# Reciprocal roots taken for two tiles at once and a new list schedule in the first layer's start, on 8 cores of a Trainium2 chip

## The chip, the cores and the metric

The kernel runs on the 8 cores of one Trainium2 chip, with the batch split over them. Each core has TensorE (PE, with its weight loads PEld), VectorE (DVE), ScalarE (ACT), GpSimd (POOL), and SyncE (SP), which issues DMA transfers. The time is that of the slowest core, in microseconds (us).

## The reference, cut to what matters

Four layers, each of this form; D_MODEL is 1024, each core has 16 prompt tiles and one sample tile of 128 tokens (17 tiles, numbered 0 to 16).

```python
h = rmsnorm(x, pre_g)                       # x * rsqrt(mean(x*x) + eps) * g
proj = einsum('bld,de->ble', h, w_in)       # columns u, v, z_a, p, z_b, xc, bg, cg, z_c
a_out, vn = chunk_gmlp(u, v, v_g, w_s, b_s) # vn = rmsnorm(v, v_g), v is 768 wide
b_out, new_pool = pool_mixer(p, ...)
c_out, new_conv = short_conv(xc, bg, cg, ...)
mix = concat([a_out * silu(z_a), b_out * silu(z_b), c_out * silu(z_c)])
x = x + rmsnorm(einsum('ble,ed->bld', mix, w_out), post_g)
```

## The kernel before, in words

The change touches only what each core does in layer 0 before its big projections start: for each of the 17 tiles, load x, normalise it, transpose it, multiply it with the v columns of w_in, and normalise the result into vn. After that come the stages of layer 0 (first the one of branch A), in which TensorE hardly ever waits, and the same again for layers 1 to 3, which are not touched.

The steps of tile j in this start, by the names that `plan_first` gives them, with engine and line of the kernel before:

- sq: ACT squares x and sums it up (L426, output `sb_samp`).
- rs: POOL adds eps (L446) and raises to the power -0.5 (L448); two instructions on one column of `stats`.
- nm: DVE multiplies x with this root and the gain into one of three buffers `hbuf` (L434).
- tp and ev: PE transposes the buffer in eight 128x128 pieces (L505), and DVE or ACT copies the result from PSUM to `hT` (L515 on DVE, L426 with output `sb_hT` on ACT). From tile N_PE_T on there is instead dt, a DMA transpose issued by SP (L518), straight from `hbuf` to `hT`.
- mm: 16 matmuls, eight pairs of 512 and 256 columns, into two PSUM banks (L528). For the first KOUT tiles they are planned as eight separate pieces mk, one for each of the eight parts of the weights w_v as these land.
- vs, vr, vn: ACT squares the product (L426, output `sb_ar`), POOL takes the root (L446, L448), DVE writes vn (L561, output `sb_mix`; the sample tile 16 goes by L434 to `sb_ar`).

Each engine runs its instructions strictly in the order written. That order is the list that `plan_first` makes: at each turn the step that could start first by its table of durations and landing times (`land_x`, `land_w`). `vbank` gives the PSUM banks: a tile's mm must wait until vn of the tile that had the banks before is done. nm of tile j waits until tile j-3 has left its `hbuf` buffer, by tp or by the landing of dt.

SP issues the loads of the x tiles in order, tile 16 once nm 4 is done, and after nm 6 in the program five loads that later stages need: `pscale`, `fac`, `convw` (8 to 36 KB), `sc_in` (480 KB) and the bias rows `b_sp` (384 KB, into `post_bc`). The DMA transposes come behind these in SP's queue. POOL issues loads too: the weight tiles `w_t` into `ring`, each behind a fixed vn (tiles 4, 5, 8 and 12 to 16), and the spatial weights `w_sp` and `w_spd` behind vn 6. Behind vn 9 DVE prepares the first weight pair (three additions, L641), behind vn 10 it masks the spatial weights, and behind vn 11 to 14 it forms sums of `hT` blocks.

Of the kernel before, what the change touches and what calls it, by code (L numbers as in the profile page):

```python
# [73 lines left out]

def plan_first():


# [9 lines left out]
    user = {}  # L87
    for j in range(NT):
        step(("sq", j), {"ACT": 1.25}, [], j + 0.0, land_x[j])
        step(("rs", j), {"POOL": 1.1}, [(("sq", j), 0.0)], j + 0.0)  # L90
# [24 lines left out]
        step(("vr", j), {"POOL": 1.1}, [(("vs", j), 0.0)], j + 1.2)  # L115
        step(("vn", j), {"DVE": 1.02}, [(("vr", j), 0.1)], j + 1.3)
    while steps:
        best = None
        for name, (engs, deps, lead, t0) in steps.items():
# [7 lines left out]
            if best is None or (t, lead) < best[0]:  # L127
                best = ((t, lead), name, eng, t + engs[eng])
        _, name, eng, end = best
# [90 lines left out]
def build_nc():  # L220
# [35 lines left out]
    with ExitStack() as es:  # L256
# [187 lines left out]
        def rstd(si):  # L444
            col = stats[:, si:si + 1]
            emit(POOL, lambda g: g.tensor_scalar(out=col, in0=col, scalar1=EPS, scalar2=None, op0=ALU.add),  # L446
                 reads=[R_stat[si]], writes=[R_stat[si]])
            emit(POOL, lambda g: g.tensor_tensor(out=col, in0=col, in1=neghalf[:], op=ALU.pow),  # L448
                 reads=[R_stat[si], R["neghalf"]], writes=[R_stat[si]])
            return col  # L450
# [1070 lines left out]
```

How the kernel before makes its waits and increments, by code:

```python
def emit(q, fn, reads=(), writes=(), dsem=None, extra=()):  # L173
# [15 lines left out]
        add(w.w)  # L189
        for tok in w.r.values():
            add(tok)
    for tok in extra:
        add(tok)
    for k, (s, v) in deps.items():
        if q.is_pe and s is q.sem:
            continue
        if q.waited.get(k, 0) >= v:
            continue
        q.h.wait_ge(s, v)
        q.waited[k] = v
    ins = fn(q.h)
    if dsem is not None:
        dsem.count += 16
        ins.then_inc(dsem.sem, 16)
        tok = (dsem.sem, dsem.count)
    else:
        q.count += 1
        ins.then_inc(q.sem, 1)
        tok = (q.sem, q.count)
    for w in writes:
        w.w = tok
# [8 lines left out]
def build_nc():  # L220
# [1225 lines left out]
            sp_dma(post_bc[:], post_g[l], [], [R["post"]], d_c["post"])  # L1446
            c_stage(l, pr)
            sp_dma(nsc_p[l], stc[:].rearrange("p a b -> p (a b)"), [R["stc"]], [], d_out)
            job = b_stage(l)
            if not last:
                load_wpg(l + 1)
            job.run()
        for dsm in d_xst + [d_out]:
            if dsm.count:
                nc.sync.wait_ge(dsm.sem, dsm.count)
    return nc
```

## Time and profile before

| what | us |
|---|---|
| median of 3 runs (lowest, highest) | 1872.65 (1869.07, 1872.83) |
| the profiled execution, its own time | 1868.77 |
| its span, from the first to the last instruction of its slowest core (7) | 1867.3 |
| spans of the eight cores in it | 1860.6 to 1867.3 |
| PE busy on core 7 | 1827.0 (98%) |
| DVE busy on core 7 | 1539.9 (82%) |

In a timeline row the first number is the start and the second how long the row lasts (several instructions of one kind are merged as "xN"); in square brackets stands how long the engine had been idle before, and what ended that.

### The profile page before, as it was taken

What the parts mean: (1) busy time and instruction counts of PE and PEld (TensorE: products, weight loads), DVE (VectorE), ACT (ScalarE), POOL (GpSimd) and SP (SyncE); (2) the same over time, 40 slices, a digit from 0 to 9 for tenths busy, and PEclk for the clock granted to TensorE, in tenths of its full rate; (3) what the DMA queues carried; (4) which work ended last, traced back from release to release, by engine and by line L of the source; (5) the groups of instructions that cost most, each with busy time, mean ns of one, the idle gap of its engine ahead of it and who ended that gap; (6) DMA issues with size and microseconds to landing.
All of it is one profiled execution on the core that took longest, in us unless ns stands there. A gap on an engine that the chain in (4) does not pass through costs nothing.

```text
span 1867.3 us, 33678 instructions; the slowest of 8 cores (1860.6 to 1867.3 us)
## 1 busy us (share of the span) xinstructions
PE 1827.0 (98%) x10048; PEld 902.7 (48%) x10048; DVE 1539.9 (82%) x2420; ACT 901.0 (48%) x1743; POOL 392.3 (21%) x698
## 2 busy tenths in 40 slices
...
GB/s 249 121 40 53 46 46 67 119 115 200 191 105 40 56 36 43 88 99 124 232 186 79 41 55 46 40 108 104 141 236 151 39 51 40 36 72 114 74 162 166
DMA packets 130979, 187.16 MB, mean 100 GB/s; under 512 B 70385, under 2 KB 76145, under 8 KB 130802
## 3 DMA queue, kind: packets, MB, share of 16 engines
...
q8 instruction: 85, 1.39, 0.3%
...
HBM read 198.79 MB, written 42.35 MB: 129 GB/s over the span
## 4 chain that ended last, share of the span: by engine, by line
PE 90%; DVE 2%; DMA 2%; issue 2%; POOL 2%; ACT 1%; SPq 0%; DVEq 0%; ACTq 0%; POOLq 0%
PE ps L656 46%; PE ps L1163 18%; PE ps L455 16%; PE ps L528 7%; PE ps L1175 1%; PE ps L747 1%; DMA sb_mix<-w_v 1%; POOL sb_stats L448 1%; PE ps L1059 1%; DVE sb_ar L434 1%; DMA sb_ar<-x_in 1%; ACT sb_ar L426 1%; DMA x_mid<-sb_ar 1%; DVE sb_ar L430 0%; POOL sb_stats L446 0%
## 5 line engine op out<-in xcount | busy, mean ns | idle before, releaser
L426 ACT ACTIVATE sb_ar<-ps 128x512 f32<-128x512 f32 (+3 forms) x774 | 489.9, 639 | 605.7 <-PE ps L656 350.5
L455 PE MATMUL ps<-sb_hT,sb_ring 128*128 128x128 bf16 (+1 forms) x2432 | 333.9, 286 | 0.2 <-DVE sb_mix L561 0.2
L656 PE MATMUL ps<-sb_wout,sb_ring 128*128 128x512 bf16 x1152 | 295.6, 379 | 0.0
L656 PE MATMUL ps<-sb_hT,sb_ring 128*128 128x512 bf16 x1152 | 295.6, 379 | 0.0
L392 POOL DMA_DIRECT2D sb_ring<-w_t x176 | 96.3, 547 | 860.1 <-PE ps L656 387.3
L430 DVE TENSOR_TENSOR sb_ar<-sb_ar 128x512 f32<-128x512 f32 (+5 forms) x332 | 256.8, 774 | 23.2 <-DVE sb_ar L430 12.9
L455 PEld LDWEIGHTS ps<-sb_hT,sb_ring 128*128 128x128 bf16 x2432 | 191.3, 98 | 154.0 <-issue 0.6
L528 PE MATMUL ps<-sb_mix,sb_hT 128*128 128x512 bf16 x1088 | 186.1, 333 | 16.7 <-DVE sb_hT L515 6.7
L1163 PE MATMUL ps<-sb_wout,sb_mix 128*128 128x512 bf16 x768 | 178.2, 379 | 4.4 <-DVE ps L1113 4.3
L448 POOL TENSOR_TENSOR sb_stats<-sb_stats,sb_neghalf 128x1 f32<-128x1 f32 x204 | 167.4, 821 | 30.6 <-POOL sb_stats L446 1.0
L656 PE MATMUL ps<-sb_wout,sb_tex 128*128 128x512 bf16 x672 | 172.4, 379 | 1.2 <-DVE sb_tex L641 1.2
L656 PEld LDWEIGHTS ps<-sb_hT,sb_ring 128*128 128x128 bf16 x1152 | 109.6, 98 | 121.2 <-issue 0.4
L430 DVE TENSOR_TENSOR sb_ar<-ps,sb_ar 128x512 f32<-128x512 f32 x240 | 163.9, 683 | 4.5 <-PE ps L656 4.4
L434 DVE SCALAR_TENSOR_TENSOR sb_ar<-sb_pcx,sb_convw,sb_ar 128x512 f32<-128x512 f32 x192 | 140.0, 749 | 24.4 <-ACT sb_ar L849 14.1
L656 PEld LDWEIGHTS ps<-sb_wout,sb_ring 128*128 128x128 bf16 x1152 | 106.7, 98 | 103.2 <-issue 0.7
L446 POOL TENSOR_SCALAR sb_stats<-sb_stats 128x1 f32<-128x1 f32 x204 | 70.9, 347 | 392.4 <-ACT sb_ar L426 302.7
L528 PEld LDWEIGHTS ps<-sb_mix,sb_hT 128*128 128x128 bf16 x1088 | 107.5, 100 | 93.4 <-issue 25.8
L656 PE MATMUL ps<-sb_wout,sb_hbuf 128*128 128x512 bf16 x480 | 123.1, 379 | 0.9 <-DVE sb_hbuf L641 0.9
L426 ACT ACTIVATE ps<-ps 128x512 f32<-128x512 f32 x176 | 103.5, 588 | 40.8 <-PE ps L1163 20.6
L1163 PEld LDWEIGHTS ps<-sb_wout,sb_mix 128*128 128x128 bf16 x768 | 74.7, 98 | 96.9 <-issue 8.9
L434 DVE SCALAR_TENSOR_TENSOR sb_ar<-ps,sb_stats,sb_post_bc 128x1024 f32<-128x1024 f32 x68 | 87.2, 1282 | 38.6 <-POOL sb_stats L448 22.4
L426 ACT ACTIVATE sb_samp<-ps 128x128 f32<-128x128 f32 (+1 forms) x152 | 61.9, 407 | 99.9 <-PE ps L1163 97.6
(115 smaller groups left out, 2191.5 us busy)
## 6 DMA issues: line engine op xcount, KB each, us to landing
...
```

Of the source, the lines that this page charges most:

```text
L392: emit(POOL, lambda g: g.dma_start(out=flat, in_=a.src), writes=a.res, dsem=d_ring[pos])
L426: return emit(ACT, lambda a: a.activation(out=out, in_=in_, func=func, scale=scale, **kw), reads=reads, writes=writes, extra=extra)
L430: return emit(DVE, lambda v: v.tensor_tensor(out=out, in0=in0, in1=in1, op=op), reads=reads, writes=writes)
L434: return emit(DVE, lambda v: v.scalar_tensor_tensor(out=out, in0=in0, scalar=scalar, in1=in1, op0=op0, op1=op1), reads=reads, writes=writes)
L446: emit(POOL, lambda g: g.tensor_scalar(out=col, in0=col, scalar1=EPS, scalar2=None, op0=ALU.add), reads=[R_stat[si]], writes=[R_stat[si]])
L448: emit(POOL, lambda g: g.tensor_tensor(out=col, in0=col, in1=neghalf[:], op=ALU.pow), reads=[R_stat[si], R["neghalf"]], writes=[R_stat[si]])
L455: ins = pe.matmul(bank(b, n), lhsT=wa.ap[:, k, :], rhs=hT[:, k, c0:c0 + n], start=(k == 0), stop=(k == 7))
L528: ins = pe.matmul(ps[:, 512 * (b + bo):512 * (b + bo) + n], lhsT=hT[:, k, j * 128:(j + 1) * 128], rhs=wv.ap[:, k, c0:c0 + n], start=(k == ...
L656: ins = pe.matmul(bank(b), lhsT=lhs[:, k, :], rhs=rhs[0][:, k, :], start=(first and k == 0), stop=(k == 3), skip_group_check=not first)
L747: ins = pe.matmul(ps[:, 512 * b + jj * 128:512 * b + (jj + 1) * 128], lhsT=vn[:, j0 + jj, h * 128:(h + 1) * 128], rhs=wsrc[:, h, :], start ...
L1059: emit(PE, lambda pe: pe.matmul(bank(b, n), lhsT=wpg[:, gi, :], rhs=dd, start=True, stop=True), reads=[rm, R["wpg"]], writes=[bank_res[b]])
L1163: ins = pe.matmul(bank(b), lhsT=lhs[0][:, k, :], rhs=rhs[:, k, :], start=(first and k == 0), stop=(k == 7), skip_group_check=not first)
```

## The change

- POOL's rs is taken for two tiles at once: tiles 0 to 4 singly, then (5, 6), (7, 8), (9, 10), (11, 12), (13, 14), (15, 16). The two instructions then work on two neighbouring columns; the tiles' sums have fixed columns of their own in `stats`.
- One tile fewer goes through TensorE's transpose: N_PE_T is 9, so tile 9 is transposed by DMA, and the banks of tiles 9 to 16 are given anew.
- Only tiles 0 and 1 have their mm in pieces (KOUT is 2). Tile 2's 16 matmuls follow as one.
- The planner has other landing times and durations, and a penalty of 0.3 on nm in its choice, so the order on every engine is another.

```diff
-N_PE_T = 10
 XSLOTS = 12
-KOUT = 3
+KOUT = 2
+N_PE_T = 9
+PEN = {"nm": 0.3}
 def vbank(j):
-    return 2 * (j % 3) if j < N_PE_T else (6, 2, 4, 0, 2, 6, 4)[j - N_PE_T]
+    return 2 * (j % 3) if j < N_PE_T else (0, 6, 2, 4, 0, 2, 6, 4)[j - N_PE_T]
+def x_pairs():
+    return [(j,) for j in range(5)] + [(j, j + 1) for j in range(5, NT, 2)]
...
-        step(("rs", j), {"POOL": 1.1}, [(("sq", j), 0.0)], j + 0.0)
+        if j == pair_of[j][0]:
+            step(("rs", j), {"POOL": 1.15}, [(("sq", i), 0.1) for i in pair_of[j]], j + 0.0)
...
-            ready = (("dt", j), 3.0)
+            ready = (("dt", j), 3.5)
...
-            if best is None or (t, lead) < best[0]:
-                best = ((t, lead), name, eng, t + engs[eng])
+            key = (t + PEN.get(name[0], 0.0), lead)
+            if best is None or key < best[0]:
+                best = (key, name, eng, t, t + engs[eng])
...
-        def rstd(si):
-            col = stats[:, si:si + 1]
+        def rstd(si, n=1):
+            col = stats[:, si:si + n]
...
-                rstd(stat_of[j])
+                rstd(NSTAT + j, next(len(p) for p in x_pairs() if j in p))
```

What this moves, at three places. All lines of the changed kernel are 8 higher here (L434 is ACT's helper there, L442 is nm, L523 ev, L569 vn).

ACT from tile 0 to tile 7, before: sq has the output `sb_samp,sb_stats`, vs has `sb_ar,sb_stats`, ev has `sb_hT`.

```order
L426 ACTIVATE sb_samp,sb_stats<-sb_ar 128x1024 x4
L426 ACTIVATE sb_ar,sb_stats<-ps 128x768 x3
L426 ACTIVATE sb_samp,sb_stats<-sb_wout 128x1024 x3
L426 ACTIVATE sb_ar,sb_stats<-ps 128x768
L426 ACTIVATE sb_samp,sb_stats<-sb_wout 128x1024 x4
L426 ACTIVATE sb_ar,sb_stats<-ps 128x768
L426 ACTIVATE sb_samp,sb_stats<-sb_wout 128x1024
L426 ACTIVATE sb_ar,sb_stats<-ps 128x768
L426 ACTIVATE sb_hT<-ps 128x8x128
```

And now:

```order
L434 ACTIVATE sb_samp,sb_stats<-sb_ar 128x1024 x4
L434 ACTIVATE sb_samp,sb_stats<-sb_wout 128x1024
L434 ACTIVATE sb_ar,sb_stats<-ps 128x768 x3
L434 ACTIVATE sb_hT<-ps 128x8x128
L434 ACTIVATE sb_samp,sb_stats<-sb_wout 128x1024 x3
L434 ACTIVATE sb_ar,sb_stats<-ps 128x768
L434 ACTIVATE sb_samp,sb_stats<-sb_wout 128x1024
L434 ACTIVATE sb_ar,sb_stats<-ps 128x768
```

sq 4 stands ahead of the first three vs; ev 3 is ACT's, where ACT had ev 7 before; vs 4 comes after sq 8 and no longer after sq 10.

DVE from tile 3 on, before: nm 3, vn 0, ev 3, vn 1 and 2, nm 4 and 5, ev 4, vn 3, ev 5, nm 6 to 8, vn 4, ev 6.

```order
L434 SCALAR_TENSOR_TENSOR sb_hbuf<-sb_ar,sb_stats,sb_pre_bc 128x1024
L561 SCALAR_TENSOR_TENSOR sb_mix<-ps,sb_stats,sb_vb_bc 128x768
L515 COPY sb_hT<-ps 128x8x128
L561 SCALAR_TENSOR_TENSOR sb_mix<-ps,sb_stats,sb_vb_bc 128x768 x2
L434 SCALAR_TENSOR_TENSOR sb_hbuf<-sb_wout,sb_stats,sb_pre_bc 128x1024 x2
L515 COPY sb_hT<-ps 128x8x128
L561 SCALAR_TENSOR_TENSOR sb_mix<-ps,sb_stats,sb_vb_bc 128x768
L515 COPY sb_hT<-ps 128x8x128
L434 SCALAR_TENSOR_TENSOR sb_hbuf<-sb_wout,sb_stats,sb_pre_bc 128x1024 x3
L561 SCALAR_TENSOR_TENSOR sb_mix<-ps,sb_stats,sb_vb_bc 128x768
L515 COPY sb_hT<-ps 128x8x128
```

And now: nm 3, nm 4, vn 0, ev 4, vn 1 and 2, nm 5 and 6, vn 3, ev 5 and 6, vn 4, nm 7 to 9, vn 5, ev 7 and 8.

```order
L442 SCALAR_TENSOR_TENSOR sb_hbuf<-sb_ar,sb_stats,sb_pre_bc 128x1024
L442 SCALAR_TENSOR_TENSOR sb_hbuf<-sb_wout,sb_stats,sb_pre_bc 128x1024
L569 SCALAR_TENSOR_TENSOR sb_mix<-ps,sb_stats,sb_vb_bc 128x768
L523 COPY sb_hT<-ps 128x8x128
L569 SCALAR_TENSOR_TENSOR sb_mix<-ps,sb_stats,sb_vb_bc 128x768 x2
L442 SCALAR_TENSOR_TENSOR sb_hbuf<-sb_wout,sb_stats,sb_pre_bc 128x1024 x2
L569 SCALAR_TENSOR_TENSOR sb_mix<-ps,sb_stats,sb_vb_bc 128x768
L523 COPY sb_hT<-ps 128x8x128 x2
L569 SCALAR_TENSOR_TENSOR sb_mix<-ps,sb_stats,sb_vb_bc 128x768
L442 SCALAR_TENSOR_TENSOR sb_hbuf<-sb_wout,sb_stats,sb_pre_bc 128x1024 x3
L569 SCALAR_TENSOR_TENSOR sb_mix<-ps,sb_stats,sb_vb_bc 128x768
L523 COPY sb_hT<-ps 128x8x128 x2
```

ev 6 now stands ahead of the three nm that it stood behind.

DVE from nm 12 on, now (nm 12, vn 7, nm 13, vn 8, nm 14, vn 9, the weight pair, nm 15, vn 10, the two masks, nm 16, vn 11):

```order
L442 SCALAR_TENSOR_TENSOR sb_hbuf<-sb_ar,sb_stats,sb_pre_bc 128x1024
L569 SCALAR_TENSOR_TENSOR sb_mix<-ps,sb_stats,sb_vb_bc 128x768
L442 SCALAR_TENSOR_TENSOR sb_hbuf<-sb_ar,sb_stats,sb_pre_bc 128x1024
L569 SCALAR_TENSOR_TENSOR sb_mix<-ps,sb_stats,sb_vb_bc 128x768
L649 TENSOR_TENSOR sb_tex<-sb_ring 128x512
L649 TENSOR_TENSOR sb_tex<-sb_tex,sb_ring 128x512
L649 TENSOR_TENSOR sb_tex<-sb_ring,sb_tex 128x512
L442 SCALAR_TENSOR_TENSOR sb_hbuf<-sb_ar,sb_stats,sb_pre_bc 128x1024
L569 SCALAR_TENSOR_TENSOR sb_mix<-ps,sb_stats,sb_vb_bc 128x768
L438 TENSOR_TENSOR sb_wmt<-sb_wmt,sb_cstb 128x768
L438 TENSOR_TENSOR sb_bdt<-sb_bdt,sb_cstb 128x768
L442 SCALAR_TENSOR_TENSOR sb_hbuf<-sb_wout,sb_stats,sb_pre_bc 128x1024
```

The same stretch before, from the weight pair on: nm 16 followed nm 15 at once, ahead of vn 10 and the masks.

```order
L641 TENSOR_TENSOR sb_tex<-sb_ring 128x512
L641 TENSOR_TENSOR sb_tex<-sb_tex,sb_ring 128x512
L641 TENSOR_TENSOR sb_tex<-sb_ring,sb_tex 128x512
L434 SCALAR_TENSOR_TENSOR sb_hbuf<-sb_ar,sb_stats,sb_pre_bc 128x1024
L434 SCALAR_TENSOR_TENSOR sb_hbuf<-sb_wout,sb_stats,sb_pre_bc 128x1024
L561 SCALAR_TENSOR_TENSOR sb_mix<-ps,sb_stats,sb_vb_bc 128x768
L430 TENSOR_TENSOR sb_wmt<-sb_wmt,sb_cstb 128x768
L430 TENSOR_TENSOR sb_bdt<-sb_bdt,sb_cstb 128x768
L561 SCALAR_TENSOR_TENSOR sb_mix<-ps,sb_stats,sb_vb_bc 128x768
```

On SP the row of DMA transposes has eight instructions where it had seven, still behind the load of `b_sp`.

## Rows read from the trace of the kernel before

**Rows 1.** Spans of all cores: us, mean granted TensorE clock.

```profile
core 3: 1866.2 us, clock 0.996
core 4: 1866.1 us, clock 0.997
core 7: 1867.3 us, clock 0.996
```

**Rows 2.** Core 7 by stage: width, busy us of each engine, clock, DMA share, GB/s.

```profile
24.00:53.00 29.00, 20.97 (x143) 12.44 (x141) 20.11 (x21) 21.00 (x42) 22.24 (x42) 0.88 0.94 264
53.00:79.00 26.00, 24.23 (x148) 14.19 (x147) 21.84 (x24) 8.40 (x19) 17.39 (x26) 1.00 0.78 110
```

**Rows 3.** Timeline of core 7, TensorE, 23 to 79 us.

```profile
23.66 1.13 PE L528 MATMUL ps<-sb_mix,sb_hT 128*128 128x512 bf16 x6 [0.27 <-DMA sb_mix<-w_v]
26.18 0.61 PE L505 MATMUL ps<-sb_cstb,sb_hbuf 128*128 128x128 bf16 x8 [1.38 <-DVE sb_hbuf L434]
28.87 4.24 PE L528 MATMUL ps<-sb_mix,sb_hT 128*128 128x512 bf16 x16 [2.08 <-DVE sb_hT L515]
...
34.61 5.40 PE L528 MATMUL ps<-sb_mix,sb_hT 128*128 128x512 bf16 x32 [0.61 <-DVE sb_hT L515]
...
44.36 7.04 PE L528 MATMUL ps<-sb_mix,sb_hT 128*128 128x512 bf16 x32 [3.46 <-DVE sb_hT L515]
...
52.79 13.16 PE L528 MATMUL ps<-sb_mix,sb_hT 128*128 128x512 bf16 x80 [0.50 <-DVE sb_hT L515]
...
70.48 7.96 PE L528 MATMUL ps<-sb_mix,sb_hT 128*128 128x512 bf16 x48 [1.20 <-DVE sb_mix L561]
78.28 1.03 PE L656 MATMUL ps<-sb_hT,sb_ring 128*128 128x512 bf16 x4
```

**Rows 4.** Timeline of core 7, VectorE, GpSimd and ScalarE, 24 to 42 us.

```profile
24.74 1.28 DVE L434 SCALAR_TENSOR_TENSOR sb_hbuf<-sb_ar,sb_stats,sb_pre_bc 128x1024 bf16<-128x1024 f32 x1 [5.43 <-POOL sb_stats L448]
...
25.30 0.80 POOL L446 TENSOR_SCALAR sb_stats<-sb_stats 128x1 f32<-128x1 f32 x1 [0.73 <-ACT sb_ar L426]
...
27.00 1.02 DVE L561 SCALAR_TENSOR_TENSOR sb_mix<-ps,sb_stats,sb_vb_bc 128x768 bf16<-128x768 f32 x1 [0.97 <-POOL sb_stats L448]
...
27.93 0.68 DVE L515 COPY sb_hT<-ps 128x1024 bf16<-128x1024 bf16 x1
...
31.88 1.39 POOL L448 TENSOR_TENSOR sb_stats<-sb_stats,sb_neghalf 128x1 f32<-128x1 f32 x1
...
41.38 1.02 ACT L426 ACTIVATE sb_hT<-ps 128x1024 bf16<-128x1024 bf16 x1
```

**Rows 5.** Core 7: SP's issues, issues with KB and us to landing, the DMA transposes.

```profile
32.11 0.62 SPq L439 DMA_DIRECT2D sb_pscale<-pscale  x1
...
34.44 0.44 SPq L439 DMA_DIRECT2D sb_post_bc<-b_sp  x1
...
sb_post_bc<-b_sp SPq DMA_DIRECT2D x1, 384.0 KB, 13.8
...
sb_pscale<-pscale SPq DMA_DIRECT2D x1, 8.0 KB, 12.5
...
DMA to landing us min/median/max: 2.8/4.2/6.6
```

**Rows 6.** Core 4: the same views (TensorE, SP, us to landing).

```profile
53.27 13.16 PE L528 MATMUL ps<-sb_mix,sb_hT 128*128 128x512 bf16 x80 [1.49 <-DVE sb_hT L515]
...
78.55 1.03 PE L656 MATMUL ps<-sb_hT,sb_ring 128*128 128x512 bf16 x4
...
34.97 1.46 SPq L439 DMA_DIRECT2D sb_post_bc<-b_sp  x1
49.65 19.47 SPq L518 DMA_TRANSPOSE sb_hT<-sb_hbuf  x7
...
sb_post_bc<-b_sp SPq DMA_DIRECT2D x1, 384.0 KB, 17.2
...
sb_hT<-sb_hbuf SPq DMA_TRANSPOSE x1, 4.7
```

More of the change, by code:

```diff
@@ L87, in plan_first @@
     user = {}
+    pair_of = {j: p for p in x_pairs() for j in p}
     for j in range(NT):
         step(("sq", j), {"ACT": 1.25}, [], j + 0.0, land_x[j])
-        step(("rs", j), {"POOL": 1.1}, [(("sq", j), 0.0)], j + 0.0)
-        gone = [] if j < NHB else [((("tp" if j - NHB < N_PE_T else "dt"), j - NHB), 0.0 if j - NHB < N_PE_T else 3.0)]
-        step(("nm", j), {"DVE": 1.28}, [(("rs", j), 0.1)] + gone, j + 0.0)
+        if j == pair_of[j][0]:
+            step(("rs", j), {"POOL": 1.15}, [(("sq", i), 0.1) for i in pair_of[j]], j + 0.0)
+        gone = [] if j < NHB else [((("tp" if j - NHB < N_PE_T else "dt"), j - NHB), 0.0 if j - NHB < N_PE_T else 3.5)]
+        step(("nm", j), {"DVE": 1.22}, [(("rs", pair_of[j][0]), 0.1)] + gone, j + 0.0)
         b = vbank(j)
@@ L97, in plan_first @@
             step(("tp", j), {"PE": 0.6}, [(("nm", j), 0.1)] + ([(("ev", j - 2), 0.1)] if j >= 2 else []), j + 0.2)
-            step(("ev", j), {"DVE": 0.7, "ACT": 1.05}, [(("tp", j), 0.1)], j + 0.3)
+            step(("ev", j), {"DVE": 0.65, "ACT": 1.0}, [(("tp", j), 0.1)], j + 0.3)
             ready = (("ev", j), 0.1)
@@ L101, in plan_first @@
             step(("dt", j), {"SP": 1.3}, [(("nm", j), 0.1)], j + 0.3)
-            ready = (("dt", j), 3.0)
-            if j == N_PE_T:
+            ready = (("dt", j), 3.5)
+            if b == 6 and j < NT - 2:
                 old = [(("ev", N_PE_T - 1), 0.1), (("ev", N_PE_T - 2), 0.1)]
@@ L114, in plan_first @@
         step(("vs", j), {"ACT": 1.0}, [(last, 0.1)], j + 1.2)
-        step(("vr", j), {"POOL": 1.1}, [(("vs", j), 0.0)], j + 1.2)
-        step(("vn", j), {"DVE": 1.02}, [(("vr", j), 0.1)], j + 1.3)
+        step(("vr", j), {"POOL": 1.15}, [(("vs", j), 0.0)], j + 1.2)
+        step(("vn", j), {"DVE": 0.95}, [(("vr", j), 0.1)], j + 1.3)
     while steps:
```

30 lines of the change are left out of this document (14 added, 16 removed).

## The prediction, made before the changed kernel ran

> **What bounds the kernel now.** I read the busy shares first: TensorE is busy nearly all of the span, so a change can only help where it waits. The stages show one such stretch before layer 0's own stages: from 24 to 53 us core 7's PE is busy 20.97 of 29.00 us at a granted clock of 0.88; from 53 to 79 us it is busy 24.23 of 26.00 at full clock [rows 2]. The change acts on these 55 us. PE's timeline then shows the waits: 2.08 us before tile 3, 0.61 before tile 4, 3.46 before tile 6, 0.50 before tile 8, all for ev, the copy of the transposed tile [rows 3]. The clock: 16 matmuls of tile 3 take 4.24 us, 32 of tiles 6 and 7 take 7.04, against 13.16/5 = 2.63 us a tile in the row of 80 [rows 3]. So two stretches run partly at half speed (1.2 GHz), each behind an idle stretch, and cost 1.6 and 1.8 us. From tile 8 on PE is nearly the bound: tile 9 begins at 52.79+2.63 = 55.4, eight tiles of 2.63 would end at 76.5, the first matmul of the next stage comes at 78.28 [rows 3]. The last 1.8 us are waits, among them 1.20 for a vn that stands late on DVE.
>
> What ends the waits is the order on the engines. ev 3 copies a tile that PE had transposed at 26.79, but stands behind vn 0 on DVE and starts at 27.93; vn 0 itself waited for vr 0, whose first POOL instruction took 0.80 us beside nm 3 [rows 3, 4].
>
> **The change part by part, on core 7.** I walk each engine's new order with the durations of the rows: nm 1.28, vn 1.02, ev 0.68 on DVE and 1.02 on ACT [rows 4], tp 0.53, tile 2.63.
>
> Tiles 2 to 4. The last part of w_v lands as now. Tiles 0 and 1 have four matmuls left (0.65 us), then all 16 of tile 2 follow: 23.66+0.65+2.63 = 26.9. That is 10 matmuls more behind the landing than the 6 now [rows 3]; they fill time in which PE idles anyway (1.38 and 2.08). tp 3 ends at 27.5. ev 3 on ACT comes behind vs 2: 27.9 to 28.9. rs 4 stands beside nm 3 and comes out at 26.8, nm 4 ends at 28.2, vn 0 at 29.1, and tile 3 needs the latter's bank: it starts at 29.2, 0.3 later than now. It then runs with tile 4 behind it, without the low clock: 29.2+5.3 = 34.5. Now tile 4 only starts at 34.61. So 2.7 us are won by here.
>
> Tiles 5 and 6. The pair step rs (5, 6) waits for sq 6, at 31.3; nm 5 and 6 end at 34.9, vn 3 at 35.8, ev 5 at 36.5, tile 5 starts at 36.6, tile 6 ends at 42.0. Now tile 6 starts at 44.36 and the low clock follows.
>
> Tiles 7 and 8. vn 5 ends at 43.4, ev 7 at 44.0, tiles 7 and 8 run from 44.3 to 49.6. Now tile 8 ends at 55.4: **5.8 us won by here**, 3.4 of them the two low-clock stretches, the rest waits.
>
> The power of two columns is not in the trace. From below it costs what one column does, 0.22+0.15+0.57 = 0.94 us with its addition; from above two of those, 1.88. I take 0.95, because the one row I have is far from a cost per element at width 1, and keep 0.9 us on the path for the upper end (it would delay nm 5, and with it tile 5). A POOL step beside an nm is longer: the power took 1.39 [rows 4]. The Trainium skill's page GPSIMD Engine Reference, section 1, says GpSimd's memory interface is shared with VectorE, with contention when VectorE has two SBUF inputs; by that the pairs nm 5/6 and nm 7 to 9 stretch vr 3 and rs 9 as nm 3 does vr 0, and the trace agrees. Without it tile 3 would start some 0.6 earlier; the sum here has it in.
>
> Tile 9 is the step at which I stop believing in the 5.8. Its dt is issued at about 41.6, when nm 9 is done; the first dt of the kernel before is issued at 49.65 on core 4 [rows 6], when the loads are nearly in. `pscale`, 8 KB, is issued at 32.11 and lands 12.5 us later, behind the x tiles issued before it; `b_sp` is issued at 34.44 and lands at 48.2 [rows 5]. SP's transfers come out in the order in which they went in. So dt 9 can't land before `b_sp`. On core 4 `b_sp` lands at 34.97+17.2 = 52.2, and the first dt, issued at 49.65, lands at 54.35, 2.2 behind it [rows 6]; the median transpose of core 7 lands 4.2 behind its issue [rows 5]. I take 2.0 behind `b_sp`, since dt 9 will have been queued longest (bounds 1 and 4.2). And `b_sp` itself comes later: the two spatial weight loads (0.38 MB) go out behind vn 6 at about 47, not at 51.7, which at 264 GB/s [rows 2] is up to 1.5 us; I take 0.8.
>
> Core 7: tile 9 starts at 48.2+0.8+2.0 = 51.0, not at 49.6. Core 4: 52.2+2.8 = 55.0, where tile 9 starts at 53.27+2.63 = 55.9 now [rows 6]: of its gain by tile 8 (it would end there at about 51.5) only 0.9 is left.
>
> From tile 9 on. Eight tiles take 21.0. nm 12 waits for the buffer of tile 9, so it starts when dt 9 lands, and behind it on DVE stand vn 7, nm 13, vn 8, nm 14, vn 9, the weight pair, nm 15, vn 10, the masks, nm 16 and vn 11: five nm at 1.2, five vn at 0.94 (they overlap by 0.09), 1.8 and 1.0, together 13.5 to 13.9. Tile 14 needs the bank that vn 11 frees and would start 13.2 after tile 9. So 0.3 to 0.7 of waiting, and I take 0.7, against 1.8 now (1.6 on core 4). vs, vr and vn of tile 16 are as now, and so are the stages after it, where PE is the bound (98% of the span busy); what is won at the end of tile 16 stays won.
>
> **The sum.** Core 7: 51.0+21.0+0.7 = 72.7 against 78.28: 5.6 less, 1867.3 becomes 1861.7. Core 4: 55.0+21.7 = 76.7 against 78.55: 1.8 less, 1866.1 becomes 1864.3. Core 3, with 1866.2 now [rows 1], lies between. So the slowest core is another one: the span falls from 1867.3 to 1864.3, by **3.0 us**. The profiled execution (1868.77) would take 1865.8; the median of the runs is 3.9 above that execution, so the forecast is 1872.65-3.0 = **1869.6**.
>
> **The rivals.**
> 1. *The DMA transposes are not held by the loads.* Then core 4 goes on from 51.5: 51.5+21.7 = 73.2, 5.3 less, 1860.8, core 7 72.7-1.4 = 71.3, 7.0 less, 1860.3. Span 1860.8, 6.5 less: 1866.2. For it: a transpose may start beside the loads' last packets on another of the 16 engines; on core 7 loads land earliest. Against it: the 12.5 us of an 8 KB load. In the Trainium skill, DMA: Bandwidth & Descriptors, section Queues, rings and completion order, completion is said not to be first in, first out for one issuing engine, although each ring is consumed in order; by its first half this rival would hold, by its second the forecast.
> 2. *The clock falls in the new gap.* On core 4 PE would idle from 51.5 to 55.0. The 3.46 us of idle before tile 6 were followed by half clock on core 7, at a cost of 1.8 [rows 3]. Then core 4 gains nothing, 1866.1, 1.2 less than now: 1871.5.
> 3. *Slower.* The queued transposes come out one by one: dt 9 4.2 behind `b_sp`, dt 10 and 11 each 2.8 later (the shortest landing [rows 5]). On core 4: dt 9 at 57.2, dt 11 at 62.8, nm 14 only then; vn 9, weight pair, nm 15, vn 10, masks, nm 16, vn 11 need 9.1 more, tile 14 starts at 71.9 and tile 16 ends at 79.8, 1.3 later than now, and 3.1 later with the clock of rival 2. Core 4: 1869.2, which is 1.9 above now: 1874.5. It decides from the point at which dt 9 lands 5 us behind `b_sp` or dt 11 10 us behind. For it: landings of up to 6.6 [rows 5]. Against it: core 4's 2.2.
>
> **How the numbers follow.** Forecast 0.50, its own range 1.5 to 4.7 less (`b_sp` delayed by 0 to 1.5, dt 9 1 to 3 behind it, two-column power at its upper end where covered). Rival 1: 0.23. Rival 2: 0.17. Rival 3: 0.10. A measurement of this kernel can't tell less than about 0.2% (3.7 us) from no change. Of the forecast's case 0.17 lies beyond that, and nearly all of rival 1; of rival 3, with the runs' own spread of 3.8 [the table of times], 0.06. Faster 0.40, same 0.54, slower 0.06. The range of 1864.5 to 1873.3 leaves out the far side of rival 1 and of rival 3.
>
> **What would show it.** Right: PE's tiles 3 and 4 back to back without low clock; tile 8 ending at about 50 to 52; then an idle stretch on PE ended by the DMA into `hT`, longest on the cores where `b_sp` lands last, and nm 12 waiting for the same; the power on two columns at about 0.57. Wrong: tile 9 directly behind tile 8 (rival 1), half clock behind the gap (rival 2), waits for each of tiles 9 to 11 (rival 3). All of it falls if `b_sp` lands before 46, or if tile 5 waits longer for its pair than computed, since sq 6 needs a tile that lands late on some cores.

## The result, and the profile after

The changed kernel takes 1877.28 us (median of 20 runs), the kernel before 1872.93 in runs beside it. The ratio is 1.0025, with a 95% interval of 1.0015 to 1.0034: **slower by 0.25%, about 4.7 us**. The medians take in all runs, the ratio only the fast ones, in which no die ran long at a lower clock. I had forecast 3.0 us less. The execution profiled took 1876.2 us. Its spans, which answer to [rows 1]:

```profile
core 0: 1860.6 us, clock 0.998
core 1: 1869.7 us, clock 0.995
core 2: 1861.0 us, clock 0.997
core 3: 1870.0 us, clock 0.995
core 4: 1861.7 us, clock 0.998
core 5: 1869.6 us, clock 0.995
core 6: 1874.9 us, clock 0.994
core 7: 1862.8 us, clock 0.997
```

Four cores (0, 2, 4, 7) are at 1861 to 1863, the other four at 1870 to 1875 with a lower clock. In this execution that split makes most of the time lost. In other executions other cores are the late ones: the median span over the executions lies between 1864.2 and 1869.9 for each of the eight cores.

I begin with the two cores of the forecast. Core 7 by stage, as in [rows 2]:

```profile
24.00:53.00 29.00, 23.73 (x156) 14.21 (x157) 21.21 (x22) 21.02 (x42) 17.80 (x32) 0.89 1.06 272
53.00:79.00 26.00, 23.68 (x143) 13.60 (x142) 21.06 (x23) 8.79 (x19) 15.60 (x25) 1.00 0.80 124
```

TensorE is busier between 24 and 53 us than before (23.73 against 20.97), but the granted clock is hardly better (0.89 against 0.88). Where the low clock lies now is seen in core 7's TensorE timeline, as in [rows 3].

```profile
22.59 0.81 PE L536 MATMUL ps<-sb_mix,sb_hT 128*128 128x512 bf16 x4 [2.04 <-DMA sb_mix<-w_v]
24.53 6.30 PE L536 MATMUL ps<-sb_mix,sb_hT 128*128 128x512 bf16 x20 [1.14 <-DMA sb_mix<-w_v]
...
33.05 5.36 PE L536 MATMUL ps<-sb_mix,sb_hT 128*128 128x512 bf16 x32 [1.33 <-ACT sb_hT L434]
...
41.27 5.36 PE L536 MATMUL ps<-sb_mix,sb_hT 128*128 128x512 bf16 x32 [1.53 <-DVE sb_hT L523]
...
49.13 7.96 PE L536 MATMUL ps<-sb_mix,sb_hT 128*128 128x512 bf16 x48 [1.61 <-ACT sb_samp L434]
57.87 10.56 PE L536 MATMUL ps<-sb_mix,sb_hT 128*128 128x512 bf16 x64 [0.78 <-DMA sb_hT<-sb_hbuf]
68.95 5.36 PE L536 MATMUL ps<-sb_mix,sb_hT 128*128 128x512 bf16 x32 [0.52 <-DVE sb_mix L569]
75.33 2.76 PE L536 MATMUL ps<-sb_mix,sb_hT 128*128 128x512 bf16 x16 [1.01 <-DMA sb_hT<-sb_hbuf]
77.92 1.03 PE L664 MATMUL ps<-sb_hT,sb_ring 128*128 128x512 bf16 x4
```

The waits up to tile 8 are smaller, as forecast: 1.33, 1.53, 1.61 before tiles 3, 5, 7, where 2.08, 0.61, 3.46 and 0.50 stood. But the 20 matmuls behind the last part of w_v (four of tiles 0 and 1, 16 of tile 2) take 6.30 us. On core 4 they take 3.41:

```profile
24.08 3.41 PE L536 MATMUL ps<-sb_mix,sb_hT 128*128 128x512 bf16 x20 [1.07 <-DMA sb_mix<-w_v]
...
46.12 5.36 PE L536 MATMUL ps<-sb_mix,sb_hT 128*128 128x512 bf16 x31 [1.56 <-DVE sb_hT L523]
56.15 14.61 PE L536 MATMUL ps<-sb_mix,sb_hT 128*128 128x512 bf16 x78 [4.67 <-DMA sb_hT<-sb_hbuf]
71.54 8.24 PE L536 MATMUL ps<-sb_mix,sb_hT 128*128 128x512 bf16 x47 [0.78 <-DVE sb_mix L569]
79.61 1.03 PE L664 MATMUL ps<-sb_hT,sb_ring 128*128 128x512 bf16 x4
```

Core 4 goes as forecast up to tile 8, which ends at 51.5. Then TensorE waits 4.67 us for the first DMA transpose (to 56.15, forecast 55.0), and the next stage starts at 79.61, where it started at 78.55 [rows 6].

Core 1 is one of the four late cores:

```profile
48.88 5.36 PE L536 MATMUL ps<-sb_mix,sb_hT 128*128 128x512 bf16 x32 [1.60 <-ACT sb_samp L434]
61.69 5.28 PE L536 MATMUL ps<-sb_mix,sb_hT 128*128 128x512 bf16 x16 [7.45 <-DMA sb_hT<-sb_hbuf]
68.03 10.56 PE L536 MATMUL ps<-sb_mix,sb_hT 128*128 128x512 bf16 x64 [1.06 <-DMA sb_hT<-sb_hbuf]
...
87.60 1.03 PE L664 MATMUL ps<-sb_hT,sb_ring 128*128 128x512 bf16 x4
```

TensorE idles 7.45 us, and tile 9's 16 matmuls take 5.28 us instead of 2.6. The stages of core 1, columns as in [rows 2]:

```profile
50.00:55.00 5.00, 4.24 (x27) 2.35 (x24) 2.48 (x3) 3.04 (x7) 3.99 (x8) 1.00 1.17 192
55.00:60.00 5.00, 0.00 (x0) 0.00 (x0) 0.00 (x0) 0.24 (x2) 1.34 (x3) 0.68 1.39 86
60.00:65.00 5.00, 3.31 (x11) 1.60 (x12) 2.21 (x2) 0.00 (x0) 0.00 (x0) 0.50 1.45 107
65.00:70.00 5.00, 3.94 (x20) 1.81 (x18) 2.01 (x2) 0.90 (x2) 1.66 (x2) 0.80 1.24 148
```

From 55 to 60 us TensorE and VectorE do nothing at all, and the granted clock falls (0.68, then 0.50). The DMA's share of busy time is at its highest (1.39 and 1.45), while it moves the least (86 and 107 GB/s): packets are in flight, but slow. Core 1's waits between 24 and 92 us (us in total, times, the longest) say who waited:

```profile
DVE sb_hbuf L442 <- DMA sb_hT<-sb_hbuf: 13.3, 2, 8.9
...
PE ps L536 <- DMA sb_hT<-sb_hbuf: 9.0, 3, 7.5
```

VectorE loses more than TensorE: nm 12 and nm 13 need the `hbuf` buffers that dt 9 and dt 10 hold until they land. Last, what else was in the DMA queues. Issues of core 1 with the us from issue to landing, each row from a narrow stretch around its issue, at 38.01 (`b_sp`), 47.99 (the second `w_t` tile, issued by GpSimd) and 46.14 (dt 9):

```profile
sb_post_bc<-b_sp SPq DMA_DIRECT2D x1, 384.0 KB, 17.3
...
sb_ring<-w_t POOLq DMA_DIRECT2D x1, 256.0 KB, 12.1
sb_hT<-sb_hbuf SPq DMA_TRANSPOSE x1, 15.1
```

So `b_sp` lands at 55.3, the `w_t` tile at 60.0 and dt 9 at 61.2. On core 7 the same transpose took 4.9 us:

```profile
sb_hT<-sb_hbuf SPq DMA_TRANSPOSE x1, 4.9
```

All cores, from the traces (us; "half clock" is how long the low clock lasts from the gap before tile 9 on, "tile 16 ends" is the start of its vn less the 2.3 us between):

| core | tile 8 ends | b_sp lands | 2nd w_t tile lands | dt 9 lands | behind b_sp | half clock | tile 16 ends, before | after | span, after less before |
|---|---|---|---|---|---|---|---|---|---|
| 0 | 53.1 | 50.6 | 55.1 | 55.1 | 4.5 | 0 | 78.3 | 78.6 | -0.1 |
| 1 | 54.2 | 55.3 | 60.0 | 61.2 | 5.9 | 10.2 | 79.2 | 87.8 | +4.2 |
| 2 | 55.2 | 51.4 | 54.8 | 52.5 | 1.1 | 0 | 81.4 | 77.0 | -3.0 |
| 3 | 52.5 | 56.3 | 57.4 | 63.2 | 6.9 | 13.7 | 77.9 | 88.3 | +3.8 |
| 4 | 51.5 | 50.0 | 55.6 | 55.8 | 5.8 | 3.4 | 78.8 | 79.9 | -4.4 |
| 5 | 54.2 | 54.8 | 59.8 | 60.4 | 5.6 | 10.2 | 77.9 | 87.6 | +8.7 |
| 6 | 53.7 | 53.9 | 59.4 | 59.4 | 5.5 | 13.6 | 77.5 | 88.9 | +14.3 |
| 7 | 54.5 | 50.2 | 54.7 | 51.3 | 1.1 | 0 | 78.5 | 78.2 | -4.5 |

Tile 16 ends at 83.3 on average where it ended at 78.7, though tile 8 ends 2.5 earlier (53.6 against 56.1). The lead or lag that a core has at the start of vn 16 stays the same to 0.3 us through 770 us, on every core but core 7 of before, so what is lost in the first 90 us stays lost. The span differs from it because single cores lose a few us in the middle of the kernel. In the execution of before core 7 loses 5.8 us between 450 and 485 us against all the others, and cores 1, 3 and 4 lose 3.6, 5.2 and 4.2 between 900 and 1000 us. After, cores 2, 6 and 7 lose 1.9, 4.1 and 2.6 behind 900 us. The cores without such a slip take 1779.4 to 1780.8 us from the start of vn 16 to their end, before and after alike. Core 7's slip in the execution of before, at a change of layer, is this:

```profile
494.99 4.21 PE L528 MATMUL ps<-sb_mix,sb_hT 128*128 128x512 bf16 x16 [3.96 <-DVE sb_ar L434]
```

VectorE had waited for a DMA transpose there, too. So the slowest core of before, core 7 with 1867.3, was the slowest by such a slip, in layers that the change doesn't touch; core 6, the slowest after, had both the late dt 9 and a slip. That slips like this hide half of what the late cores lose in the other executions too (9 to 11 us on four cores become 4.7 of the time) is argued, not shown.

### The profile page after: what moved, and what is told of

It reads as the page before. It is cut to its first block, busy times and chain, and to the rows that moved or that the text cites. A ratio compares the mean times of both kernels' runs of the same rounds, so it can differ in the third digit from the quotient of the medians.

```text
span 1874.9 us, 33612 instructions; the slowest of 8 cores (1860.6 to 1874.9 us)
## 1 busy us (share of the span) xinstructions
PE 1828.9 (98%) x10040; PEld 903.3 (48%) x10040; DVE 1538.3 (82%) x2419; ACT 901.1 (48%) x1743; POOL 392.6 (21%) x686
## 3 DMA queue, kind: packets, MB, share of 16 engines
q8 instruction: 85, 1.39, 0.3%
## 4 chain that ended last, share of the span: by engine, by line
PE 87%; DVE 3%; issue 3%; DMA 3%; POOL 2%; ACT 1%; DVEq 0%; SPq 0%; ACTq 0%; POOLq 0%
PE ps L664 45%; PE ps L1171 16%; PE ps L463 16%; PE ps L536 6%; PE ps L1183 1%; PE ps L755 1%; POOL sb_stats L457 1%; DMA sb_mix<-w_v 1%; DMA sb_hT<-sb_hbuf 1%; DVE sb_ar L442 1%; PE ps L1067 1%; DVE sb_ar L438 1%; ACT sb_ar L434 1%; DMA x_mid<-sb_ar 1%; DVE sb_hbuf L442 0%
## 5 line engine op out<-in xcount | busy, mean ns | idle before, releaser
L434 ACT ACTIVATE sb_ar<-ps 128x512 f32<-128x512 f32 (+3 forms) x774 | 489.9, 639 | 607.6 <-PE ps L664 351.8
L457 POOL TENSOR_TENSOR sb_stats<-sb_stats,sb_neghalf 128x1 f32<-128x1 f32 (+1 forms) x198 | 171.0, 864 | 29.7 <-POOL sb_stats L455 0.6
L442 DVE SCALAR_TENSOR_TENSOR sb_ar<-sb_pcx,sb_convw,sb_ar 128x512 f32<-128x512 f32 x192 | 139.9, 749 | 24.2 <-ACT sb_ar L857 14.2
L455 POOL TENSOR_SCALAR sb_stats<-sb_stats 128x1 f32<-128x1 f32 (+1 forms) x198 | 67.4, 341 | 400.9 <-ACT sb_ar L434 311.5
L434 ACT ACTIVATE ps<-ps 128x512 f32<-128x512 f32 x176 | 103.5, 588 | 41.7 <-PE ps L1171 21.2
L442 DVE SCALAR_TENSOR_TENSOR sb_ar<-ps,sb_stats,sb_post_bc 128x1024 f32<-128x1024 f32 x68 | 87.2, 1282 | 37.9 <-POOL sb_stats L457 19.6
L434 ACT ACTIVATE sb_samp<-ps 128x128 f32<-128x128 f32 (+1 forms) x152 | 61.8, 407 | 100.6 <-PE ps L1171 98.3
```

The lines of the kernel that those rows point to most:

```text
L434: return emit(ACT, lambda a: a.activation(out=out, in_=in_, func=func, scale=scale, **kw), reads=reads, writes=writes, extra=extra)
L442: return emit(DVE, lambda v: v.scalar_tensor_tensor(out=out, in0=in0, scalar=scalar, in1=in1, op0=op0, op1=op1), reads=reads, writes=writes)
```

## The experiments

All kernels compute the whole result. I had three questions: which part of the change costs, what delays dt 9, and what is left once it isn't delayed. My theory (T in the expectations) was that tile 9's transpose comes while loads are still in flight and crawls; later I narrowed it to the loads of GpSimd's queue beside it (Q). The rivals were that SP's own loads ahead of it hold it, that the spatial weights do (S), and that the pairs or the new order do the harm (P). "Tile 16" below is the mean end of tile 16 over the eight cores, and the highest; it is 78.7 and 81.4 before, 83.3 and 88.9 after. Ratios are to the kernel before, with the 95% interval, from 4 to 11 runs of each kernel. Landings and "tile 16" are read from one execution of each kernel, and loads land some us apart from one execution to the next.

### Which part costs

**Ten TensorE transposes again**, all else as changed:

```diff
-N_PE_T = 9
+N_PE_T = 10
-    return ... else (0, 6, 2, 4, 0, 2, 6, 4)[j - N_PE_T]
+    return ... else (6, 2, 4, 0, 2, 6, 4)[j - N_PE_T]
```

> The changed kernel with ten TensorE transposes again (N_PE_T 10, the old banks, list made by the changed planner); everything else as changed. Theory T (the transpose of tile 9 goes out while the loads are still landing, so it and the two behind it crawl and TensorE waits for them): tile 9 needs no DMA, the first DMA transpose is issued 4 us later and is needed 2.6 us later; the stage of branch A begins on core 1, 3, 5 and 6 at 74 to 80 us instead of 87.5 to 88.5, and the kernel is 3 to 6 us faster than the one before. Rival P (the pairs and the new order on VectorE lose the time): still slower than before by 2 to 6 us. Rival S (the spatial weights, loaded earlier, are the cause): little change from the changed kernel, landings of DMA transposes stay at up to 15 us.

Measured: 0.9993 (0.9979 to 1.0007), tile 16 at 76.9 and 78.9. The loss is gone, and tile 16 ends 1.8 before that of the kernel before; the time shows no clear gain, where I had expected 3 to 6 us. The first DMA transpose is dt 10, which lands at 52 to 58 on the cores; tile 9 covers the wait.

**Nine in the kernel before**, the same two lines the other way (and the matching condition for the banks):

> The kernel before with nine TensorE transposes alone (its own landing table, single roots; its list made anew). Theory T: tile 9's DMA transpose goes out at about 46 to 49 us, close to the last loads; slower than the kernel before by 1 to 5 us, with landings over 8 us for tiles 9 and 10 on some cores. Rival P: same as the kernel before within 1 us, since the pairs aren't there.

Measured: 1.0000 (0.9990 to 1.0011), tile 16 at 80.0 and 84.1. The mechanism is there, the loss of time that I expected is not seen. On all eight cores dt 9 lands within 0.2 us of the second `w_t` tile (58.9 and 58.9, 54.1 and 54.0, 56.8 and 56.8, 59.6 and 59.5, 53.4 and 53.6, 59.9 and 60.0, 56.5 and 56.4, 54.7 and 54.8), and 4.6 to 8.4 us behind `b_sp`. Core 5, issues at 46.59 and 45.91 (us to landing), and its TensorE:

```profile
sb_ring<-w_t POOLq DMA_DIRECT2D x1, 256.0 KB, 13.4
sb_hT<-sb_hbuf SPq DMA_TRANSPOSE x1, 14.0
```

```profile
60.12 7.01 PE L528 MATMUL ps<-sb_mix,sb_hT 128*128 128x512 bf16 x32 [4.74 <-DMA sb_hT<-sb_hbuf]
```

Here tile 8 ends later (54.8 to 58.7): on five cores dt 9 is there by then, on three TensorE waits 2.3 to 4.7 us. So harm of the changed kernel's size came only with both parts of the change: the earlier tile 8 makes a longer gap of a transpose that is late in both.

**Pairs alone** in the kernel before (its constants, banks and N_PE_T; list made anew):

```diff
+def x_pairs():
+    return [(j,) for j in range(5)] + [(j, j + 1) for j in range(5, NT, 2)]
```

> The kernel before with the pairs alone: ten TensorE transposes, its own landing times and durations, three tiles in pieces, the list made anew with pair roots. Both theories: the DMA transposes go out as before, so nothing crawls; the end of tile 8 moves by less than 2 us from 55.3 to 56.1, and the kernel stays within 2 us of the one before. If the pairs themselves cost (rival P), 2 us or more slower.

Measured: 0.9995 (0.9981 to 1.0009), tile 16 at 78.1 and 79.9, tile 8 ending at 54.1 to 58.1 (before: 55.2 to 59.1), 56.1 on average in both. The pairs alone cost nothing that is seen; they are not the loss.

### What delays the transpose

**SP's five later loads behind the last transpose**, `b_sp` first among them:

```diff
-                if j == 6:
-                    sp_dma(pscale[:], ...)   # and fac, convw, sc_in, b_sp
...
+            elif kind == "dt":
+                t_job(j, j % NHB)
+                if j == NT - 1:
+                    sp_dma(post_bc[:, 0:768], b_sp[0], ...)   # and the other four
```

> The changed kernel, but the five loads for later stages (pscale, fac, convw, sc_in, b_sp; 0.9 MB) are issued behind the last DMA transpose instead of behind nm 6. Theory T: the queue is free of them when tile 9's transpose is issued at 44 to 46 us, which then waits only for the last x tiles (45 to 47) and lands by 50 to 52; the stage of branch A begins at 73 to 77 us on all cores, kernel 3 to 7 us faster than before. Rival S: the transposes still meet the weight loads of GpSimd's queue and land 10 to 15 us behind their issue. Rival P: no change from the changed kernel.

Measured: 0.9980 (0.9970 to 0.9990), tile 16 at 76.3 and 83.7. dt 9 lands at 47 to 51, before it is needed. So SP's own loads do hold it: with them out of the way it no longer waits. It was not slowed much by GpSimd's queue either: on all eight cores the second `w_t` tile went out 1.9 us behind dt 9, and dt 9 took 3.6 to 5.1 us and landed ahead of it. But not all is gone. On core 3 dt 10 was issued at 51.5, beside a `w_t` tile (in flight to 55.6) and the spatial weights (to 61.4 and 62.2), and took this:

```profile
sb_hT<-sb_hbuf SPq DMA_TRANSPOSE x1, 10.8
```

```profile
62.38 21.20 PE L536 MATMUL ps<-sb_mix,sb_hT 128*128 128x512 bf16 x112 [4.52 <-DMA sb_hT<-sb_hbuf]
```

With no load of SP's left to blame, the transpose lands with `w_spd` of GpSimd's queue, at 62.2; the half clock follows (seven tiles in 21.20 us, not 18.4).

**Spatial weights behind vn 9** instead of vn 6:

```diff
-                elif j == 6:
+                elif j == 9:
                     load_spatial(0)
```

> The changed kernel, but the two spatial weight loads are issued behind vn 9 instead of vn 6. Rival S: the transposes land 4 to 7 us behind their issue, and the kernel is 3 to 6 us faster than before. Theory T: tile 9's transpose still lands no sooner than the load of b_sp (50 to 55 us) and at most 2 us are won on the changed kernel.

Measured: 1.0024 (0.9996 to 1.0051), tile 16 at 78.9 and 84.3. The interval is too wide for a word on the time; one run of 1895 us makes it so, the other eight in it lie between 1867.7 and 1873.4. dt 9 still lands with the `w_t` tile on three cores (59.9 and 59.8, 57.3 and 57.3, 53.6 and 53.6), so the spatial weights are not what delays dt 9; dt 10 now comes about 1 us behind dt 9 on five cores and 3.2 to 3.5 on three, where it came 4 to 8 us behind it on the late cores, on three of them within 0.2 us of `w_spd`. So they do delay dt 10.

**`w_t` tiles earlier and spatial weights later**: the second `w_t` tile is in (46.3 to 49.9) before `b_sp` is, so that hardly a load of GpSimd's is left beside dt 9, while SP's loads stay ahead of it.

```diff
-                if j in (4, 5, 8, 12, 13, 14, 15, 16):
+                if j in (2, 3, 8, 12, 13, 14, 15, 16):
                     ring_try()
-                elif j == 6:
+                elif j == 9:
                     load_spatial(0)
```

> The changed kernel, but no load of GpSimd's queue is near the transposes of tiles 9 to 11: the first two weight tiles are issued behind vn 2 and 3 (about 32 and 36 us), the spatial weights behind vn 9; the five later loads stay ahead of the transposes on SP's queue. Theory Q (a transpose crawls while a load of GpSimd's queue is in flight beside it; the two land together): tile 9's transpose lands within 3 us of the load of b_sp, at 51 to 54 us, the next ones within 2 us of each other, and the stage of branch A begins at 74 to 78 us on all cores; 2 to 5 us faster than the kernel before. Theory T alone (the loads ahead in SP's own queue): landings at 55 to 63 us as in the changed kernel, on some cores.

Measured: 0.9994 (0.9980 to 1.0008), tile 16 at 79.4 and 84.4. dt 9 lands 0.9 to 2.5 us behind `b_sp` on all eight cores and dt 10 within 1 us behind it. This is the landing that my forecast had assumed. The time shows no clear gain, though, where I had expected 2 to 5 us. Core 5's TensorE:

```profile
54.79 13.16 PE L536 MATMUL ps<-sb_mix,sb_hT 128*128 128x512 bf16 x80 [1.90 <-DMA sb_hT<-sb_hbuf]
...
79.08 5.28 PE L536 MATMUL ps<-sb_mix,sb_hT 128*128 128x512 bf16 x16 [3.77 <-DMA sb_hT<-sb_hbuf]
```

The gap before tile 9 is 1.90 at full clock. But the spatial weights now land at 64 to 68, and VectorE's masks wait for them (1.5 us on core 5), with nm 16 behind them. dt 16, issued at 68.95 on core 5 beside a `w_t` tile (issued at 67.45, landed at 73.9), takes 9.8 us and lands at 78.7, and the last tile pays 3.77 us and half clock.

**Only the `w_t` tiles earlier** (the first of the two edits):

> The changed kernel, but the first two weight tiles of GpSimd's queue are issued behind vn 2 and 3 (about 32 and 36 us) instead of vn 4 and 5; the five later loads and the spatial weights stay where the change has them. Theory Q (a transpose crawls while a load of GpSimd's queue is in flight beside it): tile 9's transpose no longer lands together with the second weight tile but 2 to 3 us behind b_sp (52 to 56 us), and tiles 10 and 11 crawl beside the spatial weights (57 to 62); the stage of branch A begins at 76 to 82 us, 0 to 4 us faster than before. Theory T: landings of tile 9 at 55 to 63 us on half of the cores, as in the changed kernel.

Measured: 1.0000 (0.9990 to 1.0009), tile 16 at 80.0 and 81.2. dt 9 lands 0.9 to 3.0 us behind `b_sp`, and dt 10 at 57 to 61, within 0.3 us of `w_spd` on seven cores. Core 5:

```profile
55.67 2.76 PE L536 MATMUL ps<-sb_mix,sb_hT 128*128 128x512 bf16 x16 [2.83 <-DMA sb_hT<-sb_hbuf]
59.93 10.56 PE L536 MATMUL ps<-sb_mix,sb_hT 128*128 128x512 bf16 x64 [1.51 <-DMA sb_hT<-sb_hbuf]
```

Against the changed kernel this edit alone takes the late cores away (highest end of tile 16 81.2 instead of 88.9) and brings the time back to that of before. It also shows a limit of my theory: on all eight cores `w_sp` and `w_spd`, GpSimd's too, were in flight when dt 9 landed (`w_sp` from 49.9 to 58.4 on core 5, where dt 9 landed at 55.2). In the changed kernel itself dt 9 landed 1.1 us behind `b_sp` on cores 2 and 7, with the second `w_t` tile in flight. A load of GpSimd's in flight is needed for the crawl of dt 9 as far as these runs go, but doesn't always bring it.

### What is left without the delay

**Ten transposes and late loads** (the edits of the first and of the fourth kernel), and **late loads in the kernel before**:

> The changed kernel with ten TensorE transposes and the five later loads behind the last DMA transpose: both cures together. Both theories: the first DMA transpose goes out at 47 to 50 us, after the x tiles are in; it lands by 55; the stage of branch A begins at 73 to 76 us on all cores, kernel 5 to 7 us faster than before. If the gain of either cure is only the other's, it stays at 3 to 4 us as with the later loads alone.

> The kernel before with only the five later loads moved behind its last DMA transpose. Theory T: its first transpose already goes out when those loads are nearly in, so at most 1 to 2 us are won (tile 13 and vn 11 wait as before); the new order of the changed kernel is what brings the rest. Rival: moving the loads is the whole gain, 3 to 4 us.

Measured: 0.9981 (0.9969 to 0.9992), tile 16 at 77.0 and 79.5; and 1.0003 (0.9994 to 1.0013), 79.6 and 81.0. The first is no better than the later loads alone (0.9980). Moving the loads brings nothing to the kernel before, so the gain of the late kernels isn't theirs; it is the new order's, once dt 9 can't undo it.

**Late loads and early `w_t` tiles**, nine transposes as changed:

> The changed kernel with the five later loads behind the last transpose and the first two weight tiles issued behind vn 2 and 3 (about 32 and 36 us), so that of GpSimd's loads only the spatial weights meet a transpose. Theory Q: the core on which tile 10's transpose took 11 us beside the second weight tile is gone; the stage of branch A begins at 73 to 77 us on all cores, 4 to 6 us faster than before. Theory T: as with the later loads alone, some cores at 79 to 84 us.

Measured: 0.9977 (0.9965 to 0.9989), median 1866.74 against 1870.16, tile 16 at 76.2 and 78.2. It beats both the kernel before and the changed one. Its ratio is the lowest of all, but those of the other kernels with late loads (0.9980 to 0.9982) lie within its interval; what it adds to them is the highest end of tile 16, 78.2 where the later loads alone had 83.7. Core 5's TensorE, where eight transposes come by DMA and none is waited for until tile 16:

```profile
48.01 18.56 PE L536 MATMUL ps<-sb_mix,sb_hT 128*128 128x512 bf16 x112 [1.74 <-DVE sb_hT L523]
67.36 5.36 PE L536 MATMUL ps<-sb_mix,sb_hT 128*128 128x512 bf16 x32 [0.78 <-DVE sb_mix L569]
73.54 2.76 PE L536 MATMUL ps<-sb_mix,sb_hT 128*128 128x512 bf16 x16 [0.82 <-DMA sb_hT<-sb_hbuf]
```

**The same with the spatial weights behind vn 4**, which I took for still better:

> The changed kernel with the five later loads behind the last transpose, the first two weight tiles behind vn 2 and 3, and the spatial weights behind vn 4 (about 41 us) instead of vn 6: all of GpSimd's early loads are under way before tile 9's transpose. Theory Q: tiles 9 to 11 land within 3 to 5 us of their issue, the stage of branch A begins at 72 to 76 us, 5 to 7 us faster than before. Rival: the earlier loads hold up the last x tiles by 1 to 2 us and the gain stays at 4 us, as with the spatial weights behind vn 6.

Measured: 0.9982 (0.9969 to 0.9996), tile 16 at 77.6 and 79.6. Not better. The spatial weights land at 49 to 53, but tile 8 ends at 52.5 to 57.0 instead of 52.3 to 54.9 and dt 9 lands at 51.4 to 55.4 (48.3 to 54.1): the last x tile comes later too, at 49.3 to 52.7 instead of 47.3 to 51.8, so the 0.38 MB went ahead of what was needed sooner.

**The same (spatial weights behind vn 6) without the pairs**:

```diff
-    return [(j,) for j in range(5)] + [(j, j + 1) for j in range(5, NT, 2)]
+    return [(j,) for j in range(NT)]
```

> The changed kernel with the later loads behind the last transpose and the first two weight tiles behind vn 2 and 3, but with single roots (the pairs undone, the list made anew). If the pairs bring something by themselves, tile 8 ends later than at 52.3 to 54.9 us (with pairs), by up to 1.5 us, and the gain on the kernel before falls from 4.3 to about 3 us; if the order and the loads are all, the same 4 us.

Measured: 1.0001 (0.9989 to 1.0013), tile 16 at 79.0 and 81.3, tile 8 ending at 54.5 to 56.3. With pairs it was 52.3 to 54.9. So of what the change wins, the pairs, with the order that they allow, bring about 2.0 us on average at tile 8 and 2.8 at tile 16, and the whole gain in time goes with them; I had expected 3 us of it to stay. Part of the 2.0 is clock: without the pairs TensorE idles 3.83 us before tile 5 (cores 0 and 5), and all eight cores have half clock for 3.4 to 6.8 us between 38 and 46 us, with them none has.

## Why the prediction was wrong, point by point

- **Tile 2 moved behind the last part of w_v.** Wrong. I counted 10 more matmuls behind the landing (they are 14: 20 against 6) as filling "time in which PE idles anyway", and did not look at what they leave behind: between 18 and 24 us TensorE was busy 5.73 us on core 7, and is busy 2.85 now. The granted clock behind it, from 24 to 30 us, was 0.87 and is 0.50 (core 7 by stage, two rows of before, then two of after):

```profile
18.00:24.00 6.00, 5.73 (x39) 3.43 (x38) 0.69 (x1) 1.15 (x2) 0.22 (x1) 1.00 0.97 289
24.00:30.00 6.00, 2.54 (x18) 1.29 (x16) 4.29 (x5) 5.57 (x11) 4.33 (x10) 0.87 0.91 319
...
18.00:24.00 6.00, 2.85 (x16) 1.19 (x14) 0.69 (x1) 1.15 (x2) 0.00 (x0) 0.97 1.03 277
24.00:30.00 6.00, 5.47 (x17) 2.49 (x18) 3.24 (x3) 2.73 (x6) 4.01 (x8) 0.50 0.91 292
```

  The 20 matmuls take 6.30 us there, and 3.41 on core 4. Tile 3 starts at 33.05 on core 7 (forecast 29.2): 2.9 of the 3.85 are this low clock, and 0.9 is the last part of w_v, which came later than in the execution of before (24.53 for 23.66). Of the 3.4 us that I had taken away with the low clock at 28.9 and 45.8, 2.9 are back at 24.5. Cores 3 and 4, with 5.86 and 3.33 us of work between 18 and 24 us, keep full clock; the other six, with 2.85 to 4.27, don't, and what sets core 4 apart I can't say.
- **Tiles 3 to 8.** Right. From tile 3's start to tile 8's end I had 20.4 us; it is 21.4 on core 7 and 20.9 on core 4, all at full clock. So of the forecast's 5.8 us by tile 8, 1.1 are left on core 7 (54.5 where it was 55.6), 4.5 are there on core 4, and 2.5 on average.
- **The power of two columns.** I took 0.95 us with its addition. Undisturbed it is 0.23+0.71 and 0.15 between them, 1.09, which is 0.15 more than one column; for two tiles that is far below two of those (1.88):

```profile
35.23 0.23 POOL L455 TENSOR_SCALAR sb_stats<-sb_stats 128x2 f32<-128x2 f32 x1 [2.25 <-ACT sb_samp L434]
35.61 0.71 POOL L457 TENSOR_TENSOR sb_stats<-sb_stats,sb_neghalf 128x2 f32<-128x2 f32 x1
```

- **dt 9 can't land before `b_sp`.** Right on all eight cores, and with `b_sp` out of the way it lands at 47 to 51. Rival 1 is thereby out; the sentence of the Trainium skill that spoke for it (DMA: Bandwidth & Descriptors, section Queues, rings and completion order: completion isn't first in, first out for one issuing engine) is not borne out by any transpose here: none overtook a load ahead of it. Its other half (each ring is consumed in order) fits.
- **`b_sp` 0.8 later.** Too little. It lands 1.5 later on average, and 1.7 to 5.7 on the four late cores, where even the x tile 16 lands at 50 us instead of 46 to 48.
- **dt 9 lands 2.0 behind `b_sp`, bounds 1 and 4.2.** This is the step that failed. It lands 1.1 to 6.9 behind it, beyond 4.2 on six cores of eight, although it was issued at 43.4 to 47.1 (forecast 41.6), before `b_sp` was in on every core. Both rows that I sized it by were of transposes issued when the loads were nearly through. The kernel before had the other case as well: on core 7 dt 12, issued at 58.3, took 2.8 us, and dt 13, issued at 59.6 beside a `w_t` load issued at 59.78, took 6.6, like the load:

```profile
sb_hT<-sb_hbuf SPq DMA_TRANSPOSE x1, 2.8
...
sb_ring<-w_t POOLq DMA_DIRECT2D x1, 256.0 KB, 6.2
sb_hT<-sb_hbuf SPq DMA_TRANSPOSE x1, 6.6
```

  I had the 6.6 in [rows 5] as the top of a spread, and never asked which transpose it was. It was the one with a load of GpSimd's beside it, and dt 9 was about to get the same company.
- **Eight tiles and 0.7 of waiting from tile 9 on.** Too small. Core 7, not held up at tile 9, still has waits of 0.78, 0.52 and 1.01, two of them for transposes (dt 10 and dt 16); so its 1.1 us of gain shrink to 0.3.
- **Which core is the slowest.** I took what is won at the end of tile 16 off the spans of cores 7, 4 and 3. Won there is won to the end, that held; but each of the three spans held a slip of 4.2 to 5.8 us behind 450 us that the change doesn't touch, so the sum began from a slowest core that the start had not made. By these figures the slowest of before would have been core 2 without slips (1864.0, tile 16 at 81.4), which I did not look at.
- **The rivals.** Rival 3 was the one that came, with its point of decision (dt 9 5 us behind `b_sp`), though not with its mechanism: the transposes don't come out one by one at 2.8 us each, core 1's land at 61.2, 67.9 and 70.0, and a load of GpSimd's beside them stood in none of my rivals. Of the five cores at 5.5 or more, core 4 lost 1.1 us and the other four 8.6 to 11.4. I had priced it at 1.3, or 3.1 with the clock, for two reasons. I worked it out on core 4, whose loads land early; and I let dt 10 follow 2.8 behind dt 9, while it came 4 to 8 behind it, beside the spatial weights that the change itself had moved there. Core 1's bill: tile 9 starts 5.8 later than before, half clock costs 2.5 on it, and some 0.2 more than before goes in what follows: 8.6, rounded. Rival 2 (half clock behind the gap) is part of it.
- **The chances.** With four of eight cores hit, and any of them able to be the slowest, a mechanism that depends on a core's loads decides the time if it strikes one core. I had summed over two cores and given it 0.10.

Two things stay open: why a core's loads come early in one execution and late in another, and why a load of GpSimd's makes a transpose crawl in most places and not in all (not beside `w_sp` where only the `w_t` tiles came earlier, not on cores 2 and 7 of the changed kernel). I tried no kernel with the same loads on another queue, so it is not shown whether it is GpSimd's queue that matters or only that more bytes are in flight.
